# Routing of the experts: choice by the eight-largest instruction, slots from one, scaling in halves, and four unread products for nine

## What is computed

```python
logits = (hf @ w_router).astype(jnp.float32)          # 256 x 8
top_v, top_i = lax.top_k(logits, TOP_K)               # 2 of 8
gates = jax.nn.softmax(top_v, axis=-1)
comb = jnp.sum(jax.nn.one_hot(top_i, N_EXPERTS, dtype=jnp.float32) * gates[..., None], axis=1)
y = jnp.zeros_like(hf)
for e in range(N_EXPERTS):
    y = y + comb[:, e:e + 1] * swiglu(hf, we_gate[e], we_up[e], we_down[e])
```

## Time and profile before

| | us |
|---|---|
| median of three runs | 1237.95 (1237.73 to 1238.04) |
| profiled execution, span from first to last instruction | 1235.0 |
| TensorE busy in it | 1213.9 (98%) |
| VectorE busy | 1006.8 (82%) |
| ScalarE busy | 820.6 (66%) |
| GpSimd busy | 57.6 (5%) |

### The profile page before, as it was taken

One profiled execution on the slowest core, in us unless ns is written; L12 is line 12 of the kernel. 1 busy time (PEld: TensorE's weight loads), 2 busy tenths in 40 slices (PEclk: granted clock), 3 DMA queues, 4 the chain that ended last, 5 costly groups with the idle time before them and its releaser, 6 DMA issues.

```text
span 1235.0 us, 16644 instructions
## 1 busy us (share of the span) xinstructions
PE 1213.9 (98%) x6709; PEld 1035.1 (84%) x6709; DVE 1006.8 (82%) x951; ACT 820.6 (66%) x753; POOL 57.6 (5%) x77
## 2 busy tenths in 40 slices
PE   8998999999999999999999999999999999999997
PEld 8987899999899788888888888888888888888885
DVE  6999654455589968989889889888888888888997
ACT  5865653344566547777778778677777777777775
POOL 4000000000100000000000000000000000000000
PEclk9999999999999999999999999999999999999999
DMA  9931555556536058999999999999999999999990
GB/s 286 345 131 52 176 183 180 196 174 200 188 137 223 18 187 290 367 371 385 377 372 380 374 385 372 373 384 373 378 386 368 382 382 365 382 385 360 398 343 36
DMA packets 182508, 359.57 MB, mean 291 GB/s; under 512 B 9174, under 2 KB 68892, under 8 KB 182428
## 3 DMA queue, kind: packets, MB, share of 16 engines
q1 hardware_dynamic: 178236, 343.25, 77.4%
q0 software_dynamic: 4176, 15.21, 3.4%
q10 hardware_dynamic: 16, 0.00, 0.0%
HBM read 350.57 MB, written 7.86 MB: 290 GB/s over the span
## 4 chain that ended last, share of the span: by engine, by line
PE 87%; DVE 8%; issue 1%; SPq 1%; DMA 1%; ACT 1%; DVEq 0%; ACTq 0%
PE YB L1888 18%; PE WBS L1867 13%; PE WBS L1869 13%; PE WBS L1868 13%; PE YB L1526 6%; PE WBS L1453 4%; PE WBS L1455 4%; PE WBS L1454 4%; DVE acc L947 3%; DVE w_lo L883 2%; PE YB L1879 2%; PE YB L1903 2%; PE YB L1507 1%; DMA raw<-in_w_in 1%; PE WBS L1487 1%
## 5 line engine op out<-in xcount | busy, mean ns | idle before, releaser
L883 DVE TENSOR_TENSOR w_lo<-raw,w_hi 128x2048 fp32r<-128x2048 f32 x324 | 736.5, 2289 | 110.0 <-ACT w_hi L546 108.5
L546 ACT ACTIVATE w_hi<-raw 128x2048 fp32r<-128x2048 f32 x324 | 617.5, 1917 | 140.9 <-PE WBS L1869 61.8
L1867 PE MATMUL WBS<-w_hi,t_hi 128*128 128x512 f32 x704 | 280.0, 398 | 0.5 <-DVE w_lo L883 0.5
L1869 PE MATMUL WBS<-w_hi,t_lo 128*128 128x512 f32 x704 | 274.9, 390 | 0.0
L1868 PE MATMUL WBS<-w_lo,t_hi 128*128 128x512 f32 x704 | 274.3, 390 | 0.0
L1867 PEld LDWEIGHTS WBS<-w_hi,t_hi 128*128 128x128 f32 x704 | 132.2, 188 | 30.5 <-issue 3.9
L1869 PEld LDWEIGHTS WBS<-w_hi,t_lo 128*128 128x128 f32 x704 | 132.1, 188 | 28.7
L1868 PEld LDWEIGHTS WBS<-w_lo,t_hi 128*128 128x128 f32 x704 | 132.4, 188 | 25.9
L1453 PE MATMUL WBS<-t_hi,w_lo 128*128 128x256 f32 x448 | 127.4, 284 | 0.0
L1454 PE MATMUL WBS<-t_hi,w_hi 128*128 128x256 f32 x448 | 126.8, 283 | 0.0
L1455 PE MATMUL WBS<-t_lo,w_hi 128*128 128x256 f32 x448 | 126.7, 283 | 0.0
(11 more groups left out here) (301 smaller groups left out, 1377.4 us busy)
## 6 DMA issues: line engine op xcount, KB each, us to landing
raw<-in_we_down SPq DMA_DIRECT2D x88, 1024.0 KB, 6.9
raw<-in_we_gate SPq DMA_DIRECT2D x80, 1024.0 KB, 6.9
raw<-in_we_up SPq DMA_DIRECT2D x80, 1024.0 KB, 7.1
raw<-in_w_in SPq DMA_DIRECT2D x20, 1024.0 KB, 5.6
raw<-in_wd_gate SPq DMA_DIRECT2D x11, 1024.0 KB, 5.2
raw<-in_wd_up SPq DMA_DIRECT2D x11, 1024.0 KB, 5.2
raw<-in_wd_down SPq DMA_DIRECT2D x11, 1024.0 KB, 4.8
raw<-in_w_out SPq DMA_DIRECT2D x8, 1024.0 KB, 8.0
```

Source lines behind the costliest of these rows:

```text
L546: act.activation(w_hi[:, hi_slot(n), :], raw[slot][:], ACT.Copy).then_inc(hi_ready, 1)
L883: dve.tensor_tensor(w_lo[slot][:], raw[slot][:], w_hi[:, hi_slot(n), :].bitcast(F32), ALU.subtract).then_inc(lo_ready, 1)
L1867: pe.matmul(bank, xs_hi[:, k0 + k, :], hi[:, k, :], start=start, stop=False)
L1869: ins = pe.matmul(bank, xs_lo[:, k0 + k, :], hi[:, k, :], start=False, stop=stop)
```

## The change

VectorE's choice is made with `max`, which gives the eight largest values of a row in order. A token's experts are those whose logit is above the second largest, or equal to it and preferred. Four pairs of instructions (one for each tile of tokens) and one comparison stand where twelve operations stood. Slots are numbered from one, so that `place` takes one operation; `before` has its diagonal, and `slot_no` starts at one. The masks of the first and the second expert apart, which the gates need, are made later, in two operations behind `sel`.

Tile 1 is scaled in two halves of 512 columns: the first stands ahead of the choice, the second behind `sel`. TensorE's `gather(0)` waits for the first half and `gather(1)` for the second. `unread(9)` becomes `unread(4)`. GpSimd writes its constants before it waits for the scaling, not behind.

```diff
-            pool.wait_ge(added, 3 * TT)
-            pool.affine_select(out=before[:], in_=ones[:], compare_op=ALU.is_gt, fill=0.0, base=0,
...
+                if l:
+                    pool.wait_ge(added, 3 * TT)
+                    pool.affine_select(out=before[:], in_=ones[:], compare_op=ALU.is_ge, fill=0.0, base=0,
...
+                    pool.iota(slot_no[:], pattern=[[1, P]], base=1, channel_multiplier=0,
...
                 pool.wait_ge(normed, TT * (2 * l + 2))
                 pool.dma_start(lnw[:], norm_weights[2 * l + 2].partition_broadcast(P)).then_inc(lnw_ready, 16)
...
-            normalize(3, 1)
...
+            dve.wait_ge(rooted, 4 * TT)
+            dve.reciprocal(rstd[:, 1:2], rstd[:, 1:2]).then_inc(inverted, 1)
+            dve.wait_ge(inverted, 4 * TT)
+            def normalize_half(half):
+                cs = slice(HALF * half, HALF * (half + 1))
+                dve.scalar_tensor_tensor(out=h[:, 1, cs], in0=X[:, 1, cs], scalar=rstd[:, 1:2], in1=lnw[:, cs],
+                                         op0=ALU.mult, op1=ALU.mult).then_inc([half_normed, normed][half], 1)
+            normalize_half(0)
             dve.wait_ge(logits_done, 1)
...
-            largest(lg, 0, first)
-            step(dve.scalar_tensor_tensor(out=l2, in0=first, scalar=NEG, in1=lg, op0=ALU.mult, op1=ALU.add))
-            largest(l2, 1, second)
-            dve.tensor_tensor(chosen, first, second, ALU.add).then_inc(choice_ready, 1)
+            for t in range(TT):
+                ins = dve.max(out=sorted_lg[:, t, :], in_=lg[:, t, :])
+            step(ins)
+            for t in range(TT):
+                ins = dve.scalar_tensor_tensor(out=first[:, t, :], in0=lg[:, t, :], scalar=sorted_lg[:, t, 1:2], in1=prefer[:, t, :],
+                                               op0=ALU.is_gt, op1=ALU.add)
+            step(ins)
+            for t in range(TT):
+                ins = dve.scalar_tensor_tensor(out=score[:, t, :], in0=lg[:, t, :], scalar=sorted_lg[:, t, 1:2], in1=first[:, t, :],
+                                               op0=ALU.is_ge, op1=ALU.mult)
+            step(ins)
+            for t in range(TT):
+                ins = dve.max(out=sorted_score[:, t, :], in_=score[:, t, :])
+            step(ins)
+            dve.tensor_tensor(chosen, score, each(sorted_score[:, :, 1:2]), ALU.is_ge).then_inc(choice_ready, 1)
...
-            step(dve.scalar_tensor_tensor(out=place, in0=YB[:, 1, 0:TT * NE].rearrange("p (t e) -> p t e", t=TT), scalar=1.0,
-                                          in1=chosen, op0=ALU.add, op1=ALU.mult))
-            step(dve.tensor_scalar(place, place, -1.0, None, ALU.add))
+            step(dve.tensor_tensor(place, YB[:, 1, 0:TT * NE].rearrange("p (t e) -> p t e", t=TT), chosen, ALU.mult))
...
             ins.then_inc(sel_ready, 1)
+            normalize_half(1)
+            step(dve.tensor_tensor(first, score, each(sorted_score[:, :, 0:1]), ALU.is_equal))
+            step(dve.tensor_tensor(second, chosen, first, ALU.subtract))
...
-            unread(9)
+            unread(4)
...
             pe.wait_ge(sel_ready, 1)
+            pe.wait_ge(normed, 3 * TT + 1)
+            pe.wait_ge(half_normed, 1)
             gather(0, YB[:, 2, :])
+            pe.wait_ge(normed, 3 * TT + 2)
             gather(1, YB[:, 3, :])
```

More of the change, by code:

```diff
@@ L140, in trunk @@
         rstd = sb("rstd", [P, TT])
+        sorted_lg = sb("sorted_lg", [P, TT, 8])
+        sorted_score = sb("sorted_score", [P, TT, 8])
         slot_of = sb("slot_of", [P, ITEMS + 1, TT])
@@ L269, in trunk @@
         y_half_done, end_hi, end_lo, end_scaled, end_root = (sem(s) for s in ("y_half_done", "end_hi", "end_lo", "end_scaled", "end_root"))
-        d_turned = sem("d_turned")
+        d_turned, half_normed = sem("d_turned"), sem("half_normed")
         logits_done, route_step, lead_exp, choice_ready, places_done, meta_ready, lead_ready = (sem(s) for s in (
@@ L455, in _ @@
             step(pool.tensor_copy(masks[:], mask_f[:]))
-            pool.memset(slot_of[:, ITEMS, :], -1.0).then_inc(consts_ready, 1)
+            pool.memset(slot_of[:, ITEMS, :], 0.0).then_inc(consts_ready, 1)
             pool.memset(gate_of[:, ITEMS, :], 0.0).then_inc(consts_ready, 1)
@@ L479, in _ @@
                 pool.dma_start(lnw[:], norm_weights[2 * l + 1].partition_broadcast(P)).then_inc(lnw_ready, 16)
+                if l:
+                    pool.wait_ge(added, 3 * TT)
+                    pool.affine_select(out=before[:], in_=ones[:], compare_op=ALU.is_ge, fill=0.0, base=0,
+                                       pattern=[[1, P]], channel_multiplier=-1).then_inc(consts_ready, 1)
+                    pool.iota(slot_no[:], pattern=[[1, P]], base=1, channel_multiplier=0,
+                              allow_small_or_imprecise_dtypes=True).then_inc(consts_ready, 1)
+                    pool.iota(token_row[:], pattern=[[1, T]], base=0, channel_multiplier=0,
+                              allow_small_or_imprecise_dtypes=True).then_inc(consts_ready, 1)
+                    pool.iota(mark[:, :, 0], pattern=[[P, TT]], base=0, channel_multiplier=1,
+                              allow_small_or_imprecise_dtypes=True).then_inc(consts_ready, 1)
                 pool.wait_ge(normed, TT * (2 * l + 2))
                 pool.dma_start(lnw[:], norm_weights[2 * l + 2].partition_broadcast(P)).then_inc(lnw_ready, 16)
-            pool.wait_ge(added, 3 * TT)
-            pool.affine_select(out=before[:], in_=ones[:], compare_op=ALU.is_gt, fill=0.0, base=0,
[L486 to L492, removed]
             for t in range(TT):
@@ L1205, in step @@
                 dve.wait_ge(route_step, steps[0])
-            eq, score, first, l2, second, comb, chosen, place, over, rank = (rout[:, k] for k in range(1, 11))
+            score, first, second, comb, chosen, place, over, rank = (rout[:, k] for k in range(1, 9))
             lead = rout[:, 12]
@@ L1216, in _ @@
             for e in range(NE):
-                ins = dve.memset(prefer[:, :, e:e + 1], float(NE - e))
+                ins = dve.memset(prefer[:, :, e:e + 1], float(NE - e) / 16.0)
             step(ins)
+            dve.wait_ge(rooted, 4 * TT)
[5 more added lines that the diff above has]
+                                         op0=ALU.mult, op1=ALU.mult).then_inc([half_normed, normed][half], 1)
@@ L1230, in _ @@
-            largest(lg, 0, first)
-            step(dve.scalar_tensor_tensor(out=l2, in0=first, scalar=NEG, in1=lg, op0=ALU.mult, op1=ALU.add))
-            largest(l2, 1, second)
-            dve.tensor_tensor(chosen, first, second, ALU.add).then_inc(choice_ready, 1)
-            step(dve.tensor_tensor(lead[:, :, 5], top[:, :, 1], top[:, :, 0], ALU.subtract))
+            for t in range(TT):
[4 more added lines that the diff above has]
+                                               op0=ALU.is_gt, op1=ALU.add)
@@ L1236, in _ @@
+            step(dve.tensor_tensor(lead[:, :, 5:6], sorted_lg[:, :, 1:2], sorted_lg[:, :, 0:1], ALU.subtract))
             dve.tensor_tensor(lead[:, :, 0], lead[:, :, 5], rstd[:], ALU.mult).then_inc(lead_ready, 1)
             dve.wait_ge(consts_ready, 6 + EXTRA)
+            dve.wait_ge(choice_ready, 1)
             dve.wait_ge(places_done, 1)
-            step(dve.scalar_tensor_tensor(out=place, in0=YB[:, 1, 0:TT * NE].rearrange("p (t e) -> p t e", t=TT), scalar=1.0,
-                                          in1=chosen, op0=ALU.add, op1=ALU.mult))
@@ L1354, in tables @@
                 if part == 4:
-                    step(dve.tensor_scalar(top[:, 0, 4:4 + EXTRA], top[:, 0, 4:4 + EXTRA], -1.0, float(NE), ALU.mult, ALU.add))
+                    step(dve.tensor_scalar(top[:, 0, 4:4 + EXTRA], top[:, 0, 4:4 + EXTRA], -16.0, float(NE), ALU.mult, ALU.add))
                     step(dve.tensor_scalar(meta[:, 1:1 + EXTRA], top[:, 0, 4:4 + EXTRA], float(NE - 1), None, ALU.min))
@@ L1814, in _ @@
             logits(1, 1).then_inc(logits_done, 1)
-            unread(9)
+            unread(4)
             pe.wait_ge(consts_ready, 3 + EXTRA)
             pe.wait_ge(choice_ready, 1)
-            ch = rout[:, 7]
+            ch = rout[:, 5]
             pe.matmul(YB[:, 1, 0:2 * NE], before[:], ch.rearrange("p t e -> p (t e)"), start=True, stop=False)
```

## The result

The changed kernel takes 1241.48 us (median of 8 runs, 1240.47 to 1242.02), the kernel before in the same runs 1237.78 (1236.86 to 1238.04). The ratio is 1.0032, with a 95% interval of 1.0023 to 1.0042. It is slower, by 3.7 us, where 1.4 us less was forecast, and outside the range. The profiled execution spans 1240.0 us for 1235.0.

What follows compares the result with a forecast made beforehand. The prediction took TensorE to bound the kernel, with DMA waiting for it. A gather starting 1.4 us sooner passed through whole: 1237.95 - 1.4 = 1236.5 us, range 1235.4 to 1239.2.

Steps and rivals of the forecast that it cites:

- The change touches only the routing, so its whole worth lies there.: Routing, about 453 to 464 us: the only part touched, worth a few us at most.
- The clock is back at 458.7.: TensorE in the routing: full clock granted again from about 458.7, as in the kernel before.
- the first rival: Routing: TensorE's clock returns late, say 462.1; gather starts at 459.95 and ends 0.35 later, 1238.3 us; chance 0.2.
- The fifth unread product starts at 456.92.: TensorE's filler ahead of the sums: after four products it is free at 456.92 and waits 0.15 for the choice.
- The choice.: VectorE's choice of experts: starts about 455.72, four pairs of 0.28 take 1.12, `chosen` starts at 456.84.
- Sums at half clock, 1.2, and one step fewer.: TensorE's sums to `place`: 1.2 at half clock; one step less (0.21) before `sel`, there at 459.0, 1.65 sooner.
- Two unread products are what is late.: TensorE ahead of the gather: two unread products end at 459.3, behind `sel`, so the gather starts 1.4 sooner.
- The cover of `t_lo`.: VectorE behind `sel`: 1.17 of added work is covered with 0.4 to spare before the first unit; caps gains at 1.8.
- GpSimd at nothing.: GpSimd writes constants some 3 us sooner, beside VectorE's copies: priced at nothing, or logits 0.1 late if copies were delayed.
- A saving in the routing is kept to the end.: Experts behind the routing: TensorE sets the pace, so the 1.4 saved ahead of the first expert passes through.

Runs made afterwards that it cites:

- the first experiment: The changed kernel with its two new small arrays placed in unused parts of rout, so other buffers keep their old addresses: 1237.31 us, ratio 0.9999.
- run 227: Not a follow-up run: the words say that the down products start 227 ns apart.
- seven and one early: The changed kernel with its new arrays in rout, seven unread products for four, and one more ahead of the turning of tile 1: 1235.12 us, ratio 0.9982.

## Why the prediction was wrong

- **"The change touches only the routing, so its whole worth lies there."** This step failed, and it is most of the miss of 5.0 us. The change also declares two arrays ahead of others, and their 128 bytes move `dT` and `eT` against the weights. The same gap without the change costs 3.7 us. The change without the gap gains 0.3 (1237.31 for 1237.58, within the noise) for the forecast 1.4, which is the other 1.1. The prediction priced every instruction of the diff and put its two declarations at nothing, without a word.
- **The clock is back at 458.7.** Also wrong. It stayed at half until 463.9 in the profiled execution, where the first rival had 462.1, or 463.4 with the late start. That rival's numbers hold there: it put the gather at 459.95, which with the 1.32 us of late start is 461.27 (measured 461.26), and the first unit 0.35 later than before (measured 0.41). The prediction gave it 0.2 and should have given it more. In its place the runs showed that whether the clock falls, and where, differs between executions of the same instructions, and that four unread products lose 2.1 us against nine. The place of the fall, on which forecast and rivals are built, was that of one execution. With seven unread products and full clock throughout, the gather starts at 459.30 and the first unit at 463.34, where the forecast for four had 459.3 and 463.35; that is luck, since the routing starts 0.6 later there and no part of it runs at half clock.
- **"The fifth unread product starts at 456.92."** A misreading of rows 7. The first four start at 455.50, 456.07, 456.50 and 456.92, so the fifth starts at 457.35, 0.43 apart again. By the prediction's own sum TensorE is then free after the choice (457.08) and not before it, and the first sum and all behind it come some 0.3 later. This decided nothing: in the changed kernel the first two of the four ran before the clock fell (457.10), the fourth started at 457.83, and `chosen`, there at 458.42, came last.
- **The choice.** The two MAX pairs take 0.25 and 0.24, as the 0.17 each of the nearest row made them. The two pairs of lines 1243 and 1247 were mis-sized: they take 0.36 each, where a pair of the other small operations takes 0.25, so the choice took 1.35 (456.90 to 458.25) for 1.12. The first sum was expected at 458.42, late start included, and came at 458.57.

```profile
456.90 0.25 DVE L1240 MAX8 sorted_lg<-YB 128x8 f32<-128x8 f32 x2
457.19 0.36 DVE L1243 SCALAR_TENSOR_TENSOR rout<-YB,sorted_lg,rout 128x8 f32<-128x8 f32 x2
...
458.25 0.17 DVE L1253 TENSOR_TENSOR rout<-rout,sorted_score 128x16 f32<-128x16 f32 x1
```

- **Sums at half clock, 1.2, and one step fewer.** Right: from the first sum to `place` 1.12 (458.57 to 459.69), `sel` 0.21 behind.
- **Two unread products are what is late.** Right: `sel` was there at 460.38, and the gather waited for them until 461.26.
- **The cover of `t_lo`.** Right, and never needed: before the first `t_lo` VectorE waited 1.66 us for ScalarE, which waited for the slow gather.
- **GpSimd at nothing.** Right: its constants stand at 454.33 to 455.22, and VectorE's two copies of the turned tile beside them take 1.52, as they did before without them (0.68 and 0.69 with a wait between, 452.85 to 454.38).
- **A saving in the routing is kept to the end.** Right: the first and the third unit are behind by the same 1.7, and with seven unread products the first and the third unit start 1.4 sooner than before (463.34 for 464.74, 469.57 for 470.97) and the span is 1.3 shorter (1233.7 for 1235.0).

## What to carry to other kernels

A declaration is a part of a change: where a new small array stands ahead of matmul operands, compare the length of untouched matmul groups before anything else, and put such arrays behind or in holes. A filler on TensorE is worth what its clock gives back to the work behind it, so it is cut by experiment over several runs and not by the wait it covers; here seven were as good as nine, and four lost 2 us. If untouched code is slower by a steady amount per repetition, look at layout and not at the edited stage.

## What the runs showed of the hardware

- The down products run 227 ns apart if their stationary operand starts at the same place within 256 bytes as the weights do (shifts of 0 and 256, or both moved by 128), which reads as a median length of 389 ns. With a relative shift of 64 or 128 bytes the medians are 392 to 396 ns, and a down product takes some 3.4 ns more on average, an estimate from 3.3 us over 960. Whether it is the weights that the stationary operand must lie alike to, or another buffer, and which of the two weight buffers, was not tried, nor were shifts other than 64, 128 and 256. Why it is so stays open.
- The granted clock of TensorE falls in the routing in some executions and not in others. In the profiled ones it was at half from 455.3 to 458.7 before, from 457.1 to 463.9 after, from 458.3 to 461.7 in the first experiment, and not at all in those of the kernels with nine, seven or six unread products on top of it (with seven and one early it fell at 455.7 for 3.4 us). Among kernels with the very instructions of the one before, and only a gap more, it fell at 455.8 (gap of 256 bytes), 457.1 (128), 459.9 (128 ahead of `eT_hi`), 459.9 (128 ahead of all) and 461.9 (64), for 3.4 us each time. Ahead of the fall in the kernel before lay turns of 128 columns, logits of 8 columns and a gap of 0.35 us, and in the first experiment four unread products and a wait of 0.67 as well. The same turns and logits were followed by no fall in the profiled executions with nine, seven and six.
- MAX over eight values in a partition takes as long as the other small operations of VectorE here (0.17, a pair 0.25). SCALAR_TENSOR_TENSOR of 128x8, whose scalar is read from a tile for each partition, takes more (0.22, a pair 0.36).
